# Squares of six output tiles added up on VectorE before the cross-partition sum, in a two-model transformer kernel

## The chip, the cores and the metric

The kernel runs on 1 core of one Trainium2 chip, in fp32 throughout. The metric is the device time in microseconds of one execution. Lower is better. The kernel before takes 3071.33 us (median of 3 runs, 3070.69 to 3072.82).

## What is computed

Two small transformer stacks of two layers each run one after the other on 256 latent and 256 context tokens with D = 1024. Their mixers are latent attention (MLA), a gated recurrence (HGRN2), an attention and pooling mixer ("even") and a neighbourhood attention ("odd"); their second halves are two SwiGLU feed-forwards and two mixtures of 32 experts. What matters here is what joins one half to the next. Every half ends in an output product, is gated into the residual stream x, and the next half begins with an RMS norm of x over the 1024 features:

```python
def rmsnorm(x, g):
    xf = x.astype(jnp.float32)
    y = xf * lax.rsqrt(jnp.mean(xf * xf, axis=-1, keepdims=True) + EPS)
    return (y * g.astype(jnp.float32)).astype(x.dtype)

x = x + g1 * y                                   # y: the mixer's output product
h2 = modulate_2(rmsnorm(x, norm_ffn_g[l]), sh2, sc2)   # h * (1 + scale) + shift
```

The mean of the squares is over all 1024 features of each token.

## The kernel before

The activations lie with features on the partitions: `X[:, k, :]` is feature tile k (128 features) of 8 (`KD = 8`) by up to 512 tokens (`T = 512`; `S = 256` is the latent half alone, `P = 128`). Summing squares over the features is then a sum over the partitions and over the 8 tiles. TensorE does both: a matmul of a matrix of ones (`ONES`) with the squared tile in `WORK[:, k * T:k * T + t]`, accumulated over k in PSUM bank 0.

`boundary` (L411) writes the join of two halves, as one part for each engine; it is called seven times. Six of the calls have a `product`, the output product of the half before; one (ahead of the odd mixer, after the first expert pass) has none. `tp` is the token width of the product, `t` that of the norm:

- MLA to feed-forward 1: tp 512, t 512
- feed-forward 1 to HGRN2: tp 512, t 512
- HGRN2 to feed-forward 2: tp 256, t 256
- feed-forward 2 to even mixer: tp 256, t 512 (the second model's context comes in here)
- even mixer to experts 1: tp 512, t 512
- odd mixer to experts 2: tp 256, t 256

They are called wide-wide (three times), narrow-narrow (twice) and narrow-wide (once) below.

The product runs over its weights in tiles of two input blocks (L451 is the matmul), eight PSUM banks being open at once, one for each output tile m. In the last weight tile (L475) m is the outer loop: two matmuls complete bank m and raise `product_made`. From then on four engines work in a chain for each m. VectorE (L517, one instruction per 256 tokens) gates the bank into `X[:, m]` and raises `added`. ScalarE (L491) squares `X[:, m]` into `WORK` and raises `squared`. TensorE (L460, `add_squares`) multiplies the square by `ONES`; that matmul for tile m - 2 is written into TensorE's program order behind the two product matmuls of tile m, for m of 2 to 7, and those of tiles 6 and 7 come last. The matmul for tile 7 raises `summed`. Then ScalarE takes the square root (L493), VectorE the reciprocal (L523) and the scaling of the eight tiles (L527), ScalarE adds the shift (L498), and TensorE starts on the next half as each normalised tile is `normed`. All engines execute their own instructions in order. SyncE waits for `product_made` to reach 8 and then issues the next half's loads (`rest`: L569, L1496, L1072, L1921 and behind it L2039); in the two expert joins GpSimd waits for it too.

Of the kernel before, what the change touches and what calls it, by code (L numbers as in the profile page):

```python
# [10 lines left out]
ALU = mybir.AluOpType  # L11
# [7 lines left out]
KD = D // P  # L19
S = 256  # L20
T = 2 * S
# [140 lines left out]
def build(nc, io, out):  # L162
    act_, dve_, pe_ = nc.scalar, nc.vector, nc.tensor
# [8 lines left out]
    WORK = sb("WORK", [P, KD * T])  # L172
# [27 lines left out]
    def sig(name):  # L200
        if name not in signals:
            signals[name] = Signal(nc, name)
        return signals[name]
# [3 lines left out]
    for name in ("inputs_in", "stored", "dve_step", "act_step", "squared", "summed", "rooted", "normed",  # L207
                 "silu_made", "h_made", "drained", "projected",
                 "scored", "peaked", "exped", "shared", "flipped", "turned", "weighted", "carried",
                 "staged", "gated", "forgot", "logged", "summed_up", "decayed", "spread", "levelled",  # L210
                 "levels_ready", "kx_flipped", "kx_copied", "state_made", "state_copied", "products",
                 "attended", "biased", "bias_in", "pooled", "pool_copied", "mixed",
                 "token_flipped", "token_copied", "routed", "group_exped", "second_exped", "ranked",
                 "rank_in", "picked", "gathered", "indices_made", "indexed", "rows_kept", "index_seen", "logits_kept", "logits_flipped", "expert_silu", "expert_h",
                 "pick_flipped", "pick_copied", "scattered", "added", "rounds_in",
                 "cleared", "mod_flipped", "inverted", "second_in", "cvec_in", "consts_in", "x_in", "late_in",
                 "silued", "chunk_made", "gained", "latent_made", "latent_squared", "latent_rooted", "latent_normed",
                 "latent_flipped", "latent_copied", "unit_made", "value_copied", "unit_squared", "unit_summed",
                 "unit_rooted", "unit_normed", "unit_flipped", "unit_copied", "mod_added",
                 "bounded", "q_made", "queried", "valued", "scanned", "level_exped", "read_in", "masked", "cross_made",  # L220
                 "cross_copied", "row_made", "row_kept", "row_squared", "row_summed", "row_rooted", "row_normed", "row_flipped", "row_copied",
                 "gains_in", "wide_in", "wide_silued", "dotted", "product_made", "out_squared", "out_rooted", "out_normed", "out_flipped", "out_copied",
                 "chunk_in0", "chunk_in1", "chunk_in2", "chunk_in3",
                 "xg_copied", "h_flipped", "h_copied", "y_copied", "weighed"):
        sig(name)
# [5 lines left out]
    def passed(**counts):  # L231
        for name, n in counts.items():
            signals[name].passed(n)
# [177 lines left out]
    def boundary(product, gain, layer, shift, scale, t, free, rest, sides=()):  # L411
# [3 lines left out]
        def of(name, n):  # L415
            return signals[name].sem, at[name] + n
# [29 lines left out]
        def pe_part(pe):  # L446
            def multiply(s, i, turn, first):
                pe.wait_ge(*of(f"loaded{s}", 16 * (turn + 1)))
                for r in range(2):
                    for m in range(KD):  # L450
                        last = pe_.matmul(PB[:, m, 0:tp], tile(s, 2, D)[:, r, m * P:(m + 1) * P],  # L451
                                          src(2 * i + r), start=first and r == 0, stop=False)
                last.then_inc(used[s].sem, 1)

            def add_squares(k):
                if product or k % 2 == 0:
                    pe.wait_ge(*of("squared", k + 1 if product else k // 2 + 1))
                else:
                    pe.wait_ge(*of("staged", k // 2 + 1))
                last = pe_.matmul(PB[:, 0, 0:t], ONES, WORK[:, k * T:k * T + t], start=k == 0, stop=k == KD - 1)  # L460
                if k == KD - 1:
                    last.then_inc(sig("summed").sem, 1)

            if product:
                multiply(0, 0, 0, True)
                with pe.Fori(0, pairs) as i:
                    for j in range(2):
                        multiply((1 + j) % 2, 2 * i + 1 + j, i + (1 + j) // 2, False)
                for i in tail[:-1]:
                    multiply(i % 2, i, i // 2, False)  # L470
                i = n_tiles - 1
                pe.wait_ge(*of(f"loaded{final}", 16 * (i // 2 + 1)))
                for m in range(KD):
                    for r in range(2):
                        last = pe_.matmul(PB[:, m, 0:tp], tile(final, 2, D)[:, r, m * P:(m + 1) * P],  # L475
                                          src(2 * i + r), start=False, stop=r == 1)
                    last.then_inc(sig("product_made").sem, 1)
                    if m >= 2:
                        add_squares(m - 2)
                add_squares(KD - 2)  # L480
                add_squares(KD - 1)
            else:
                for k in range(KD):
                    add_squares(k)
# [16 lines left out]
        def dve_part(dve):  # L501
            for share in side_shares(sides):
                side_dots(dve, of, sides, share, 0, 11)
            if not product:
                for k in range(1, KD, 2):
                    dve_.tensor_tensor(WORK[:, k * T:k * T + t], X[:, k, 0:t], X[:, k, 0:t], ALU.mult) \
                        .then_inc(sig("staged").sem, 1)
            for w in range(streams):
                last = dve_.scalar_tensor_tensor(
                    out=GAIN[:, w, :], in0=MODS[:, layer, KD * scale:KD * scale + KD, w], scalar=1.0, in1=gain,  # L510
                    op0=ALU.add, op1=ALU.mult)
            last.then_inc(sig("gained").sem, 1)
            if product:
                for m in range(KD):
                    dve.wait_ge(*of("product_made", m + 1))
                    for c in range(tp // S):
                        last = dve_.scalar_tensor_tensor(  # L517
                            out=X[:, m, half(c)], in0=PB[:, m, half(c)], scalar=piece(gate_layer, gate, m, c),
                            in1=X[:, m, half(c)], op0=ALU.mult, op1=ALU.add)
                    last.then_inc(sig("added").sem, 1)  # L520
            dve.wait_ge(*of("gained", 1))
            dve.wait_ge(*of("rooted", 1))
            dve_.reciprocal(ROOT[:, 0, 0:t], ROOT[:, 0, 0:t]).then_inc(sig("inverted").sem, 1)  # L523
            dve.wait_ge(*of("inverted", 1))
            for k in range(KD):
                for w in range(streams):
                    last = dve_.scalar_tensor_tensor(out=A[:, k, half(w)], in0=X[:, k, half(w)], scalar=GAIN[:, w, k:k + 1],  # L527
                                                     in1=ROOT[:, 0, half(w)], op0=ALU.mult, op1=ALU.mult)
                last.then_inc(sig("spread").sem, 1)
# [12 lines left out]
        for s in range(2 if product else 0):  # L542
            count = (n_tiles + 1 - s) // 2
            used[s].passed(count - (s == final))
            loaded[s].passed(16 * count)
        passed(product_made=KD if product else 0, added=KD if product else 0, squared=KD if product else KD // 2,
               staged=0 if product else KD // 2, summed=1, rooted=1, gained=1, inverted=1, spread=KD, normed=KD)
        return Boundary(sp_part, pe_part, act_part, dve_part, ready, multiplied)

# [1873 lines left out]
    def nothing(sp):  # L2423
# [3 lines left out]
    opening(mla_early)  # L2427
    product = mla(0)
    product = feed_forward(boundary(product, vec("norm2", 0, KD), 0, 3, 4, T, feed_free((1, 2)), feed_rest(w13[0], (1, 2))),
                           w13[0], w2[0], 0, T, sides=(1, 2))  # L2430
    product = hgrn2(boundary(product, vec("norm1", KD, 2 * KD), 1, 0, 1, T, hgrn2_head(1), hgrn2_head(0),
                              (1, 2)), 1)
    product = feed_forward(boundary(product, vec("norm2", KD, 2 * KD), 1, 3, 4, S, feed_free((3,)),
                                    feed_rest(w13[1], (3,), True)), w13[1], w2[1], 1, S, True, sides=(3,))
    product = even_mixer(boundary(product, vec("mix", 0, KD), 2, 0, 1, T, even_free, even_rest, (3,)), 2)
    experts(boundary(product, vec("ffn", 0, KD), 2, 3, 4, T, nothing, experts_early(0)), 2, 0, T, True)
    product = odd_mixer(boundary(None, vec("mix", KD, 2 * KD), 3, 0, 1, T, nothing, odd_early), 3)
# [109 lines left out]
```

## Time and profile before

| what | value |
|---|---|
| median of 3 runs | 3071.33 us (3070.69 to 3072.82) |
| the profiled execution | 3070.39 us, of which the span is 3068.6 us |
| granted TensorE clock, mean of the span | 0.968 |
| TensorE busy | 2847.9 us (93%), 12390 instructions |
| VectorE busy | 1163.6 us (38%) |
| ScalarE busy | 701.3 us (23%) |
| L475, the last weight tile of the six products | 192 matmul records |
| L460, the sums of squares of the seven joins | 112 matmul records |

An fp32 matmul appears as two records, so L460's 112 records are 56 matmuls: 8 in each of seven joins. In the timeline a row gives start, length, engine, line, what is written and read, how many instructions are merged into it and, in brackets, how long the engine was idle before and what released it. "PEld" rows are weight loads of TensorE, "SPq" rows are DMA issues of SyncE. The granted clock is 1.00 for 2.4 GHz and 0.50 for 1.2 GHz.

### The profile page before, as it was taken

Reading aid. Unit: us, or ns where it says so; the run is one execution under the profiler, and the core shown is the slowest. Engines: PE = TensorE matmul, PEld = TensorE weight load, DVE = VectorE, ACT = ScalarE, POOL = GpSimd, SP = SyncE. Lnnn points to the kernel's source line nnn. Section 1 sums busy time; section 2 is a strip of 40 time slices with the busy share of each in tenths; the row PEclk is TensorE's granted clock in tenths of the full one; section 3 lists DMA queues with packets and bytes.
Section 4 is the critical chain, followed back from the end, with each engine's and each line's share of the span. In section 5 each row is a group of like instructions: output and inputs, shape, how many; then the busy total and the mean of one; then the engine's idle time right before and its main releaser. Section 6 shows DMA issues by size and latency. Waiting matters only on the chain. (4 is left out here: it accounts for less than half of the span.)

```text
span 3068.6 us, 34189 instructions
## 1 busy us (share of the span) xinstructions
PE 2847.9 (93%) x12390; PEld 1568.3 (51%) x12390; DVE 1163.6 (38%) x2597; ACT 701.3 (23%) x1331; POOL 20.1 (1%) x26
## 2 busy tenths in 40 slices
PE   5999999999999988999989799999979979999997
PEld 3545444444467767887553333333347764444443
DVE  2322387770256664762232333323334322112222
ACT  2333200000155541001151112112123222112121
POOL 0000000000000000000000000000000000000000
PEclk9979999999999988999999899999999989999999
DMA  6122365551222105774003899999912249999993
GB/s 250 71 97 109 145 239 226 225 219 69 110 83 71 68 1 191 304 269 164 14 11 133 330 396 394 391 396 398 364 55 90 95 161 403 398 392 400 397 399 135
DMA packets 101826, 664.39 MB, mean 217 GB/s; under 512 B 10608, under 2 KB 19056, under 8 KB 25072
## 3 DMA queue, kind: packets, MB, share of 16 engines
q1 hardware_dynamic: 98576, 651.74, 54.3%
q0 software_dynamic: 2592, 9.44, 0.8%
q10 hardware_dynamic: 576, 2.10, 0.2%
q8 instruction: 54, 0.88, 0.1%
q14 instruction: 28, 0.23, 0.0%
HBM read 660.09 MB, written 3.15 MB: 216 GB/s over the span
## 5 line engine op out<-in xcount | busy, mean ns | idle before, releaser
L618 PE MATMUL PB<-A,RING 128*128 128x512 f32 (+1 forms) x1408 | 458.4, 489 | 9.8 <-ACT A L498 6.2
L618 PEld LDWEIGHTS PB<-A,RING 128*128 128x128 f32 x1408 | 269.3, 191 | 199.0 <-issue 174.7
L400 DVE SCALAR_TENSOR_TENSOR WORK<-RING,MORE 128x1024 f32<-128x1024 f32 x288 | 335.5, 1220 | 21.1 <-ACT MORE L632 11.8
L451 PE MATMUL PB<-BIG,RING 128*128 (+2 forms) x928 | 310.7, 497 | 5.5 <-PEq L586 3.3
L2293 DVE TENSOR_TENSOR BIG<-BIG,PB 64x512 f32<-64x512 f32 x64 | 44.2, 690 | 711.1 <-ACT BIG L2207 711.1
L2138 PE MATMUL PB<-BIG 128*128 128x512 f32 (+1 forms) x544 | 213.3, 515 | 49.1 <-DVE X L2300 45.6
L451 PEld LDWEIGHTS PB<-BIG,RING 128*128 128x128 f32 x928 | 175.9, 190 | 139.2 <-issue 128.6
L2106 PE MATMUL PB<-RING,BIG 128*64 128x512 f32 x1024 | 227.7, 597 | 0.0
L2300 DVE SCALAR_TENSOR_TENSOR X<-PB,MODS,X 128x256 f32<-128x256 f32 x408 | 176.6, 479 | 42.7 <-PE PB L2138 40.7
L2138 PEld LDWEIGHTS PB<-BIG 128*128 128x128 f32 x544 | 90.9, 190 | 184.6 <-DVE X L2300 107.3
L517 DVE SCALAR_TENSOR_TENSOR X<-PB,MODS,X 128x256 f32<-128x256 f32 x72 | 32.6, 480 | 357.7 <-PE PB L475 357.7
L2106 PEld LDWEIGHTS PB<-RING,BIG 128*64 128x64 f32 x1024 | 72.4, 138 | 138.2 <-issue 137.8
L2207 ACT ACTIVATE BIG<-PB 64x512 f32<-64x512 f32 x64 | 37.7, 589 | 364.9 <-PE PB L2106 364.9
L1596 PE MATMUL PB<-A,RING 128*128 128x512 f32 x256 | 114.5, 602 | 6.2 <-ACT A L498 6.2
L2218 ACT ACTIVATE BIG<-PB 64x512 f32<-64x512 f32 x128 | 75.8, 592 | 193.7 <-PE PB L2126 192.9
L2126 PE MATMUL PB<-RING,BIG 128*64 128x512 f32 x512 | 116.9, 598 | 1.8
L491 ACT ACTIVATE WORK<-X 128x512 f32<-128x512 f32 (+1 forms) x52 | 29.0, 563 | 390.6 <-DVE X L517 390.6
L637 ACT ACTIVATE RS<-PB 128x512 f32<-128x512 f32 (+1 forms) x44 | 21.6, 491 | 420.7 <-PE PB L618 420.7
L2126 PE MATMUL PB<-A,BIG 128*64 128x512 f32 x512 | 116.9, 598 | 0.0
L2106 PE MATMUL PB<-MORE,BIG 128*64 128x512 f32 x512 | 115.4, 592 | 0.0
L2106 PE MATMUL PB<-CST,BIG 128*64 128x512 f32 x256 | 115.4, 592 | 0.0
L2106 PE MATMUL PB<-BIG 128*64 128x512 f32 x256 | 115.1, 592 | 0.0
(350 smaller groups left out, 3387.0 us busy)
## 6 DMA issues: line engine op xcount, KB each, us to landing
RING<-moe_w SPq DMA_DIRECT2D x192, 1024.0 KB, 8.3
RING<-ada_rows SPq DMA_DIRECT2D x72, 1024.0 KB, 6.8
RING<-ffn_w SPq DMA_DIRECT2D x66, 1024.0 KB, 4.8
MORE<-moe_w SPq DMA_DIRECT2D x64, 1024.0 KB, 8.8
A<-moe_w SPq DMA_DIRECT2D x64, 1024.0 KB, 7.4
CST<-moe_w SPq DMA_DIRECT2D x32, 1024.0 KB, 8.9
BIG<-moe_w SPq DMA_DIRECT2D x32, 1024.0 KB, 10.8
RING<-ada_w SPq DMA_DIRECT2D x17, 1024.0 KB, 6.4
```

What stands on the lines that cost most here:

```text
L400: dve_.scalar_tensor_tensor(out=JUNK[:, n % 4, :], in0=RING[:, s, b * D:(b + 1) * D], scalar=1.0, in1=WIDE[:, side // 2, w, :], op0=ALU.mu ...
L451: last = pe_.matmul(PB[:, m, 0:tp], tile(s, 2, D)[:, r, m * P:(m + 1) * P], src(2 * i + r), start=first and r == 0, stop=False)
L517: last = dve_.scalar_tensor_tensor(out=X[:, m, half(c)], in0=PB[:, m, half(c)], scalar=piece(gate_layer, gate, m, c), in1=X[:, m, half(c)] ...
L618: last = pe_.matmul(PB[:, 2 * s + j, 0:t], tile(s, KD, P, j * KD * P)[:, k, :], A[:, k, 0:t], start=k == 0, stop=k == KD - 1)
L1596: last = pe_.matmul(PB[:, 1 + d, :], w[:, k, :], A[:, k, :], start=k == 0, stop=k == KD - 1)
L2106: last = pe_.matmul(PB[m * CAP:(m + 1) * CAP, 0, :], XGT[:, b, k, slots_of(e % 2)], spot_tile(s, 4, T)[:, k % 4, :], start=k == 0, stop=k ...
L2126: last = pe_.matmul(PB[m * CAP:(m + 1) * CAP, 2, :], HB[:, e % 2, k, :], spot_tile(s, 2, D)[:, k % 2, m * T:(m + 1) * T], start=k == 0, st ...
L2138: pe_.matmul(PB[:, 6 + m % 2, 0:t], Y2[:, b, m * P:(m + 1) * P], SWT[:, 0:t], start=True, stop=True) \
L2207: act_.activation(HS[CAP:P, e % 2, :], PB[0:CAP, 0, :], ACT.Silu).then_inc(sig("expert_silu").sem, 1)
L2218: last = act_.activation(Y2[slots_of(e % 2), b, m * T:(m + 1) * T], PB[m * CAP:(m + 1) * CAP, 2, :], ACT.Copy)
L2293: dve_.tensor_tensor(HS[0:CAP, j, :], HS[CAP:P, j, :], PB[CAP:P, 0, :], ALU.mult) \
L2300: last = dve_.scalar_tensor_tensor(out=X[:, m, half(w)], in0=PB[:, 6 + m % 2, half(w)], scalar=piece(2 + moe, 5, m, w), in1=X[:, m, half(w ...
```

## The change

In joins with a product, VectorE adds the squared tiles 0 to 5 up in place, in `WORK[:, 0:t]`, by five `tensor_tensor` adds. The add in step m (m of 2 to 6) comes behind L517 of tile m; it waits for the square of tile m - 1 and for the add before it, and raises `piled`. TensorE no longer has any sum of squares between the product matmuls. Behind the last of them it waits for the fifth `piled`, multiplies the pile by `ONES`, and then squares 6 and 7 as before. The join without a product is as it was.

```diff
             def add_squares(k):
-                if product or k % 2 == 0:
+                if k == 0 and product:
+                    pe.wait_ge(*of("piled", KD - 3))
+                elif product or k % 2 == 0:
                     pe.wait_ge(*of("squared", k + 1 if product else k // 2 + 1))
                 else:
                     pe.wait_ge(*of("staged", k // 2 + 1))
@@
                     last.then_inc(sig("product_made").sem, 1)
-                    if m >= 2:
-                        add_squares(m - 2)
+                add_squares(0)
                 add_squares(KD - 2)
                 add_squares(KD - 1)
@@
                     last.then_inc(sig("added").sem, 1)
+                    if 2 <= m < KD - 1:
+                        dve.wait_ge(*of("squared", m))
+                        dve.wait_ge(*of("piled", m - 2))
+                        dve_.tensor_tensor(WORK[:, 0:t], WORK[:, 0:t], WORK[:, (m - 1) * T:(m - 1) * T + t], ALU.add) \
+                            .then_inc(sig("piled").sem, 1)
```

The rest of the diff adds the semaphore `piled` to the list of names and counts its 5 steps in `passed`.

## Rows read from the trace of the kernel before

**Rows 1.** The page, part 1: busy time and share of the span.

```profile
PE 2847.9 (93%) x12390; PEld 1568.3 (51%) x12390; DVE 1163.6 (38%) x2597; ACT 701.3 (23%) x1331; POOL 20.1 (1%) x26
```

**Rows 2.** The page, part 5: L517, busy, mean ns, idle before and its releaser.

```profile
L517 DVE SCALAR_TENSOR_TENSOR X<-PB,MODS,X 128x256 f32<-128x256 f32 x72 | 32.6, 480 | 357.7 <-PE PB L475 357.7
```

**Rows 3.** Timeline, first wide-wide join (all engines).

```profile
336.99 5.31 PE L475 MATMUL PB<-BIG,RING 128*128 128x512 f32 x12
...
345.57 1.88 PE L475 MATMUL PB<-BIG,RING 128*128 128x512 f32 x4
...
347.29 1.02 PE L460 MATMUL PB<-WORK,CST 128*128 128x512 f32 x2
...
355.01 2.92 PE L460 MATMUL PB<-WORK,CST 128*128 128x512 f32 x6
...
355.22 0.87 DVE L517 SCALAR_TENSOR_TENSOR X<-PB,MODS,X 128x256 f32<-128x256 f32 x2 [1.70 <-PE PB L475]
...
356.12 0.63 ACT L491 ACTIVATE WORK<-X 128x512 f32<-128x512 f32 x1 [1.95 <-DVE X L517]
356.80 0.30 PEld L460 LDWEIGHTS PB<-WORK,CST 128*128 128x128 f32 x2 [0.74 <-ACT WORK L491]
357.97 0.69 ACT L493 ACTIVATE RS<-PB,CST 128x512 f32<-128x512 f32 x1 [1.22 <-PE PB L460]
358.76 3.35 DVE L523 RECIPROCAL RS<-RS 128x512 f32<-128x512 f32 x1 [2.67 <-ACT RS L493]
```

**Rows 4.** Waits of SyncE's DMA queue, whole span: total us, times, longest.

```profile
SPq L1921 <- PE PB L475: 47.0, 2, 31.4
SPq L569 <- PE PB L475: 43.8, 2, 29.1
SPq L1496 <- PE PB L475: 29.6, 1, 29.6
SPq L1072 <- PE PB L475: 14.9, 1, 14.9
```

**Rows 5.** Timeline, second narrow-narrow join (all engines).

```profile
2499.80 0.48 DVE L517 SCALAR_TENSOR_TENSOR X<-PB,MODS,X 128x256 f32<-128x256 f32 x1 [21.69 <-PE PB L475]
...
2500.66 0.48 DVE L517 SCALAR_TENSOR_TENSOR X<-PB,MODS,X 128x256 f32<-128x256 f32 x1 [0.38 <-PE PB L475]
...
2502.82 0.48 DVE L517 SCALAR_TENSOR_TENSOR X<-PB,MODS,X 128x256 f32<-128x256 f32 x1 [0.81 <-PE PB L475]
...
2504.12 0.48 DVE L517 SCALAR_TENSOR_TENSOR X<-PB,MODS,X 128x256 f32<-128x256 f32 x1 [0.81 <-PE PB L475]
...
2507.80 1.03 PE L460 MATMUL PB<-WORK,CST 128*128 128x256 f32 x4
...
2508.99 0.70 PE L460 MATMUL PB<-WORK,CST 128*128 128x256 f32 x2 [0.16 <-ACT WORK L491]
```

**Rows 6.** Timeline, first narrow-narrow join: start of the next half.

```profile
1200.62 7.57 PE L618 MATMUL PB<-A,RING 128*128 128x256 f32 x26 [3.67 <-DMA RING<-ffn_w]
```

**Rows 7.** Timeline, narrow-wide join.

```profile
1432.82 1.02 PE L460 MATMUL PB<-WORK,CST 128*128 128x512 f32 x2
...
1436.27 2.74 PE L460 MATMUL PB<-WORK,CST 128*128 128x512 f32 x6
```

**Rows 8.** Timeline of VectorE: adds and products of two tensors, elsewhere.

```profile
408.59 0.69 DVE L647 TENSOR_TENSOR BIG<-PB,RS 128x512 f32 x1 [1.36 <-ACT RS L637]
409.19 1.22 DVE L400 SCALAR_TENSOR_TENSOR WORK<-RING,MORE 128x1024 f32<-128x1024 f32 x1
...
1212.94 0.42 DVE L647 TENSOR_TENSOR BIG<-PB,RS 128x256 f32 x1 [0.36 <-DVE WORK L400]
1213.29 1.22 DVE L400 SCALAR_TENSOR_TENSOR WORK<-RING,MORE 128x1024 f32<-128x1024 f32 x1
...
2260.81 2.50 DVE L506 TENSOR_TENSOR WORK<-X 128x512 f32<-128x512 f32 x4 [4.06 <-PEq L2372]
```

**Rows 9.** Busy by stretch after two joins; columns: length, engines, PEclk, DMA, GB/s.

```profile
366.00:368.00 2.00, 2.00 (x4) 0.96 (x3) 2.00 (x6) 2.00 (x6) 0.00 (x0) 0.50 0.32 135
368.00:370.00 2.00, 2.00 (x5) 0.76 (x4) 0.57 (x2) 1.98 (x5) 0.00 (x0) 0.88 0.00 0
...
1198.00:1200.00 2.00, 0.00 (x0) 0.00 (x0) 1.96 (x3) 0.13 (x1) 0.00 (x0) 1.00 0.99 406
```

More of the change, by code:

```diff
@@ L221, in build @@
                  "cross_copied", "row_made", "row_kept", "row_squared", "row_summed", "row_rooted", "row_normed", "row_flipped", "row_copied",
-                 "gains_in", "wide_in", "wide_silued", "dotted", "product_made", "out_squared", "out_rooted", "out_normed", "out_flipped", "out_copied",
+                 "gains_in", "wide_in", "wide_silued", "dotted", "product_made", "piled", "out_squared", "out_rooted", "out_normed", "out_flipped", "out_copied",
                  "chunk_in0", "chunk_in1", "chunk_in2", "chunk_in3",
@@ L545, in boundary @@
             loaded[s].passed(16 * count)
-        passed(product_made=KD if product else 0, added=KD if product else 0, squared=KD if product else KD // 2,
+        passed(product_made=KD if product else 0, added=KD if product else 0, piled=KD - 3 if product else 0, squared=KD if product else KD // 2,
                staged=0 if product else KD // 2, summed=1, rooted=1, gained=1, inverted=1, spread=KD, normed=KD)
```

## Prediction

> **What bounds the kernel now.** Read the busy shares first. TensorE is busy for 93% of the span and the other engines for 38% or less [rows 1]. So time taken out of TensorE's own order counts where nothing else ends later, and the joins must be read one by one. L517 is the next view: all its idle time, 357.7 us, ended with TensorE's product [rows 2]. VectorE is early at every join and TensorE sets the pace.
>
> The timeline of a join shows that pace. In the wide-wide join, four records of L475 (two matmuls) take from 345.57 to 347.29, that is 0.43 us a record and 0.86 us for a matmul of 512 columns [rows 3]. The product's last tile begins at 336.99 and its last matmul gives way to L460 at 355.01 [rows 3]: 18.02 us, or 21 matmuls of 0.86. Sixteen are the product; five are squares 0 to 4. Those five lie ahead of the event that everything waits for. The squares 5 and 6, started at 355.01, lie beside L517 and L491 of tile 7 and cost nothing: the weight load for square 7 waits for ScalarE until 356.80, after 0.74 us of idle loading [rows 3].
>
> The next half hangs on that event too. SyncE's issues L569, L1496, L1072 and L1921 (L2039, the experts' weights, stands behind L1921) all waited for L475 [rows 4]. So transfers move with the product's end, and no stream of loads has a fixed start that would swallow the gain.
>
> **The change part by part.** *Removed from the path:* five matmuls in each of six joins. Wide-wide: 5 x 0.86 = 4.3 us, three times, 12.9 us. Narrow-narrow: without a square two L517 stand 0.86 us apart (2499.80, 2500.66), with one 1.30 us (2502.82, 2504.12) [rows 5]; a 256-column square is 0.43 to 0.44 us. 5 x 0.43 = 2.15 us, twice, 4.3 us. Narrow-wide: its squares are 512 columns wide. From 1432.82 to 1436.27, two rounds of two narrow product matmuls (0.86) and one square (0.86), 3.45 us, bear this out [rows 7]. 4.3 us. Sum: 21.5 us. The squares left behind the product are still three (pile, 6, 7) where they were three (5, 6, 7).
>
> *Added on VectorE:* five adds in each of the six joins, from and to SBUF. Durations: a two-tensor instruction of 512 columns takes 0.69 us, of 256 columns 0.42 [rows 8]. What counts is how soon the next can start. L400, behind L647 and with waits of its own that had been met, started 0.60 us after it (408.59, 409.19) in the wide case and 0.35 us after it in the narrow one (1212.94, 1213.29); four L506 of 512 columns from SBUF took 2.50 us, so 0.60 apart [rows 8]. Two L517 of 0.48 us (mean 480 ns [rows 2]) took 0.87 [rows 3], so they start 0.39 to 0.40 apart. I take these spacings (0.60, 0.35, 0.40) and not the full lengths, since L400 is in the same position as L517 behind the new add: another kind of instruction, a satisfied wait ahead of it.
>
> VectorE per tile against TensorE per tile, once the squares are out:
> - Wide-wide: 2 x 0.40 + 0.60 = 1.40 us against 2 x 0.86 = 1.72. TensorE still sets the pace. The fifth add begins 0.2 + 0.8 = 1.0 us after tile 6 is made (L517 starts 0.2 us behind its matmuls, 355.22 against 355.01 [rows 3]) and ends at 1.7, as tile 7 is made. TensorE's wait then costs 0.05 to 0.1 us for the event and 0.1 for the weight load, and the pile and square 6 end 1.85 to 1.9 us after the product's end. Square 7 could not start before 356.80 - 355.01 = 1.8 us plus its load [rows 3]. Cost on the path: 0.
> - Narrow-narrow: 0.40 + 0.35 = 0.75 against 0.86. The fifth add ends 0.2 + 0.4 + 0.42 = 1.0 us after tile 6 is made, 0.16 after tile 7. The pile starts some 0.3 us late, pile and square 6 end at 0.3 + 0.86 = 1.2 us, and square 7 cannot start before 2508.99 - 2507.80 = 1.19 us [rows 5]. Cost: 0, with nothing to spare.
> - Narrow-wide: 0.40 + 0.60 = 1.00 against 0.86. Here VectorE becomes the bound. It falls 0.14 us back per tile. L517 of tile 6 starts 0.2 + 4 x 0.14 = 0.76 us after its tile is made, the add 0.4 later, ends 0.69 later, and TensorE starts 0.15 behind that: 2.0 us after tile 6, 1.15 us after tile 7 is made. Then come the pile and square 6 (1.72 us) and square 7 (1.02 us with its drain), 3.89 us after the product's end where now it is 2.74 [rows 7]. Cost: 1.15 us, so this join gains 3.15.
>
> *The waits:* the add in step m waits for the square of tile m - 1, and L517 of tile m + 1 is queued behind it. ScalarE ends that square 0.90 + 0.63 = 1.53 us after L517 of tile m - 1 began (355.22 to 356.12, and 0.63 long) [rows 3]; the wide-wide add is not reached before 1.72 + 0.80. In the narrow-wide join L517 has half the length, so the square ends 1.15 us after it began and the add is reached at 1.40. Both waits are met before. The wait on the add before is older still. No DMA is issued, moved or removed.
>
> *Downstream:* in the first narrow-narrow join the next half began with the landing of its weights (L618 released by DMA at 1200.62 [rows 6]); that transfer is issued at the product's end and moves with it, by the full 2.15 us.
>
> **Sum:** 12.9 + 4.3 + 3.15 = 20.35 us. The profiled execution took 3070.39 us (span 3068.6 plus 1.8 around it), 0.94 below the median, so by it 3050.0; from the median, 3071.33 - 20.35 = 3051.0. I predict the latter.
>
> **The clock** can move this by chance. TensorE is idle while VectorE makes the reciprocal, and afterwards works at 1.2 GHz (0.50) for some time: in the first join until within 368 to 370 us [rows 9]. In the first narrow-narrow join the clock was still 1.00 in idle time (1198 to 1200) [rows 9]. Where the fall and rise lie against the work changes when the work moves; a slow stretch longer or shorter by 2 us costs or gives 1 us at each of six joins. My estimate of the sum is 3 us either way. The new idle in the narrow-wide join (1.15 us) is shorter than idle that left the clock whole.
>
> **The rivals.**
> - *VectorE is held until each instruction has ended.* Then the periods are 0.88 + 0.04 + 0.69 + 0.04 = 1.65 us (wide-wide), 0.98 (narrow-narrow) and 1.25 (narrow-wide). Wide-wide loses 0.1 us; narrow-narrow falls 0.12 us back per tile, 0.6 us at tile 7; in the narrow-wide join the pile starts 2.28 us after the product, a cost of 2.3. Gain 12.6 + 3.1 + 2.0 = 17.7, time 3053.6 us. Against it: 0.60 and 0.35 us from start to start [rows 8], though none of those instructions reads what the one before last wrote. This is also a rule of the Trainium skill, "VectorE: DVE Perf Modes", section "The DRAIN you can't avoid": the next instruction does not start until the pipeline is empty, with or without semaphores. By that rule the time is 3053.6 us; the trace, with 0.60 us against a length of 0.69, does not agree.
> - *The adds cost far more than their rows (slower).* The accumulation in place in `WORK`, while ScalarE writes and TensorE reads other parts of it, might be much slower than L506. The price goes by the slowest row of this width, the reciprocal's 3.35 us [rows 3], some 1.75 us if half as wide. VectorE per tile is then 4.15, 2.15 and 3.75 us; the pile would start 12.5, 6.7 and 14.8 us after the product, and the joins would lose 8.0, 4.3 and 10.5 us net: 43 us in all, 3114 us. It decides against the change where an add costs some 1.1 us more than its row. For it speaks only that no row adds in place; against it every two-tensor row of 512 columns I read, from PSUM or SBUF.
> - *The gain is given back in the expert passes.* If their weight stream set their end from a start before the product, the gains of the last two joins (4.3 + 2.15) would be hidden, 3057.5 us, and by the same reasoning at more joins under 0.2% would be left. Against it L2039 stands behind L1921, which waits for the product [rows 4].
>
> **How the numbers follow.** Measurement can tell about 0.2% (6 us) from no change. Forecast 0.70 (3051.0), held VectorE 0.17 (3053.6), gain given back 0.09 (3057.5 for 0.04 of it, less than 6 us gained for 0.05), slow adds 0.04 (3114). Faster 0.91, same 0.05, slower 0.04. The range takes in 20.35 us and 17.7 us with 3 us of clock on the far side of each, and a little of the rest: 3046.5 to 3057.5.
>
> **What would show it.** L460 should fall from 112 records to 52. In the wide-wide joins L475 should be one row of 32 records, 13.7 us long, with L460 directly behind it and VectorE's adds 0.69 us long; L517 of tile 7 should begin 0.2 us behind the product. In the narrow-wide join TensorE should be idle about 1.15 us ahead of the pile. L517 spaced over 0.9 us in the narrow-narrow joins would show VectorE held. Idle before L460 of over a microsecond in the wide-wide joins would show the adds to be dearer; a longer idle before L618 or L2106 with DMA as the releaser, a gain given back.

## The result

The changed kernel takes 3052.0 us (median of 4 runs, 3051.63 to 3052.27), where the kernel before took 3071.43 beside it (4 runs): ratio 0.9933, 95% interval 0.9918 to 0.9949, 15.7 to 25.2 us less. (The ratio compares all runs of the two kernels, taken side by side, and need not be the quotient of the medians, here 0.9937.) The forecast was 3051.0. The profiled execution has a span of 3049.8 us.

**The page after**, parts 1 and 5, where [rows 1, 2] answer. L517 has become L518.

```profile
PE 2831.5 (93%) x12330; PEld 1557.8 (51%) x12330; DVE 1179.3 (39%) x2627; ACT 700.8 (23%) x1331; POOL 20.2 (1%) x26
...
L518 DVE SCALAR_TENSOR_TENSOR X<-PB,MODS,X 128x256 f32<-128x256 f32 x72 | 32.6, 481 | 322.4 <-PE PB L477 321.9
```

TensorE has 60 records fewer (30 matmuls) and 16.4 us less busy time, VectorE 30 instructions and 15.7 us more. Thirty matmuls fewer should be worth 21.5 us; in the six joins TensorE is indeed busy for 77.4 us instead of 98.4, and the difference to 16.4 lies ahead of the first join (299.9 us busy, before 297.2) and between the joins. VectorE's idle time ahead of the gating fell by 35.3 us: it waits less, but TensorE is still what it waits for.

**Timeline of the first wide-wide join**, all engines, where [rows 3] answer. L477 is the product, L525 the add, L462 the sum of squares, L494 the square root.

```profile
338.76 13.90 PE L477 MATMUL PB<-BIG,RING 128*128 128x512 f32 x32
...
349.26 0.88 DVE L518 SCALAR_TENSOR_TENSOR X<-PB,MODS,X 128x256 f32<-128x256 f32 x2 [0.24 <-PE PB L477]
350.05 0.68 DVE L525 TENSOR_TENSOR WORK<-WORK 128x512 f32<-128x512 f32 x1
...
350.97 0.88 DVE L518 SCALAR_TENSOR_TENSOR X<-PB,MODS,X 128x256 f32<-128x256 f32 x2 [0.24 <-PE PB L477]
352.50 2.91 PE L462 MATMUL PB<-WORK,CST 128*128 128x512 f32 x6
...
352.69 0.88 DVE L518 SCALAR_TENSOR_TENSOR X<-PB,MODS,X 128x256 f32<-128x256 f32 x2 [0.24 <-PE PB L477]
353.60 0.63 ACT L492 ACTIVATE WORK<-X 128x512 f32<-128x512 f32 x1 [1.09 <-DVE X L518]
354.28 0.30 PEld L462 LDWEIGHTS PB<-WORK,CST 128*128 128x128 f32 x2 [0.62 <-ACT WORK L492]
355.45 0.69 ACT L494 ACTIVATE RS<-PB,CST 128x512 f32<-128x512 f32 x1 [1.22 <-PE PB L462]
```

The product is one unbroken row of 32 records. The add begins 0.79 us after the first of its tile's two gating instructions, and VectorE is idle for 0.24 us before the next tile: it keeps up. The load for square 7 still waits for ScalarE (354.28), as at 356.80 before [rows 3], so the pile and square 6 lie beside VectorE and ScalarE and cost nothing. Start of the product tile to square root: 16.69 us, before 20.98.

**The narrow-wide join**, where [rows 7] answer:

```profile
1417.37 7.07 PE L477 MATMUL PB<-BIG,RING 128*128 128x256 f32 x32
...
1423.15 0.48 DVE L518 SCALAR_TENSOR_TENSOR X<-PB,MODS,X 128x256 f32<-128x256 f32 x1
1423.54 0.69 DVE L525 TENSOR_TENSOR WORK<-WORK 128x512 f32<-128x512 f32 x1
...
1424.14 0.48 DVE L518 SCALAR_TENSOR_TENSOR X<-PB,MODS,X 128x256 f32<-128x256 f32 x1
...
1425.28 2.84 PE L462 MATMUL PB<-WORK,CST 128*128 128x512 f32 x6 [0.84 <-DVE WORK L525]
...
1428.16 0.69 ACT L494 ACTIVATE RS<-PB,CST 128x512 f32<-128x512 f32 x1 [1.88 <-PE PB L462]
```

From the first add on no L518 has idle time before it: VectorE is the bound, with 0.99 to 1.00 us per tile (1423.15, 1424.14), and TensorE waits for the fifth add.

**The first narrow-narrow join and the start of the next half**, where [rows 5, 6] answer:

```profile
1180.64 7.07 PE L477 MATMUL PB<-MORE,RING 128*128 128x256 f32 x32
...
1186.03 0.48 DVE L518 SCALAR_TENSOR_TENSOR X<-PB,MODS,X 128x256 f32<-128x256 f32 x1
...
1186.89 0.48 DVE L518 SCALAR_TENSOR_TENSOR X<-PB,MODS,X 128x256 f32<-128x256 f32 x1
1187.29 0.42 DVE L525 TENSOR_TENSOR WORK<-WORK 128x256 f32<-128x256 f32 x1
...
1187.76 1.68 PE L462 MATMUL PB<-WORK,CST 128*128 128x256 f32 x6
...
1189.48 0.47 ACT L494 ACTIVATE RS<-PB,CST 128x256 f32<-128x256 f32 x1 [0.79 <-PE PB L462]
...
1193.01 3.33 PE L624 MATMUL PB<-A,RING 128*128 128x256 f32 x7 [3.57 <-ACT A L499]
```

The gatings begin 0.86 us apart (1186.03, 1186.89), TensorE's pace. L624's matmul (L618 before) is released by ScalarE here, and not by DMA as in [rows 6]; the second profile of the kernel before, below, has ScalarE there too, so this difference is not the change's doing.

All six joins, from the start of the product's last weight tile to the start of the square root, in us, each worked out from two timeline rows:

| join | before | after | gain | forecast |
|---|---|---|---|---|
| wide-wide 1, 2, 3 | 20.98, 20.98, 20.99 | 16.69 each | 4.29, 4.29, 4.30 | 4.3 each |
| narrow-narrow 1, 2 | 10.99, 10.99 | 8.84 each | 2.15 each | 2.15 each |
| narrow-wide | 13.97 | 10.79 | 3.18 | 3.15 |
| sum | 98.90 | 78.54 | 20.36 | 20.35 |

The spans differ by 18.8 us, the medians by 19.4. The rest lies outside the joins: in these two profiles the stretch ahead of the first join, in which nothing was changed, is 336.99 us before and 338.76 after.

### The profile page after: what moved, and what is told of

The parts are those of the page before. It is cut to its first block and busy times, and to the rows that moved or that the text cites. A ratio compares the mean times of both kernels' runs of the same rounds, so it can differ in the third digit from the quotient of the medians.

```text
span 3049.8 us, 34130 instructions
## 1 busy us (share of the span) xinstructions
PE 2831.5 (93%) x12330; PEld 1557.8 (51%) x12330; DVE 1179.3 (39%) x2627; ACT 700.8 (23%) x1331; POOL 20.2 (1%) x26
## 3 DMA queue, kind: packets, MB, share of 16 engines
HBM read 660.09 MB, written 3.15 MB: 217 GB/s over the span
## 5 line engine op out<-in xcount | busy, mean ns | idle before, releaser
L624 PE MATMUL PB<-A,RING 128*128 128x512 f32 (+1 forms) x1408 | 458.8, 489 | 9.8 <-ACT A L499 9.8
L624 PEld LDWEIGHTS PB<-A,RING 128*128 128x128 f32 x1408 | 269.5, 192 | 199.1 <-issue 174.8
L400 DVE SCALAR_TENSOR_TENSOR WORK<-RING,MORE 128x1024 f32<-128x1024 f32 x288 | 335.6, 1222 | 21.5 <-ACT MORE L638 11.3
L518 DVE SCALAR_TENSOR_TENSOR X<-PB,MODS,X 128x256 f32<-128x256 f32 x72 | 32.6, 481 | 322.4 <-PE PB L477 321.9
```

Of the source, the lines that this page charges most:

```text
L400: dve_.scalar_tensor_tensor(out=JUNK[:, n % 4, :], in0=RING[:, s, b * D:(b + 1) * D], scalar=1.0, in1=WIDE[:, side // 2, w, :], op0=ALU.mu ...
L518: last = dve_.scalar_tensor_tensor(out=X[:, m, half(c)], in0=PB[:, m, half(c)], scalar=piece(gate_layer, gate, m, c), in1=X[:, m, half(c)] ...
L624: last = pe_.matmul(PB[:, 2 * s + j, 0:t], tile(s, KD, P, j * KD * P)[:, k, :], A[:, k, 0:t], start=k == 0, stop=k == KD - 1)
```

## The experiments

"Stretches" below are the times from one join's square root to the next join's last weight tile, the sixth being the one to the end; the stretch ahead of the first join is kept apart. "Half-clock time" is worked out from the view of busy time by stretch, in pieces of 20 us: length times two times (1 - granted clock), summed, which is the time at 1.2 GHz.

### The same two kernels again

> The kernel before, once more, for a second profile of the same program. What it tells apart: whether the stretches between the joins, in which the two kernels do the same work, repeat from one execution to the next. If the 1.0 us by which the measured gain (19.4 us) lies under the gain of the six joins (20.4 us) is chance of the clock in those stretches, then stretches of 200 to 800 us differ by 0.2 to 1.2 us between two profiles of this one kernel, in both directions. If the change itself costs something outside the joins, the stretches of this kernel repeat within 0.1 us and those of the changed kernel stand apart. Time: 3071 us.

> The changed kernel, once more, beside the others. Time 3052.0 us, ratio 0.9937. Each join from the start of the last weight tile to the square root as in the first profile: 16.69 us wide-wide, 8.84 us narrow-narrow, 10.79 us narrow-wide, to within 0.05 us, since nothing in a join depends on chance; the stretches between the joins by up to 1.2 us otherwise than in the first profile.

The six joins repeated within 0.02 us (sums 98.89 and 78.52). The changed kernel: 3050.9 us, ratio 0.9932 (0.9915 to 0.9949). The stretches repeated better than I expected, within 0.03 us for the changed kernel and 0.41 us for the kernel before, whose single execution here took 3076.25 us where I had expected 3071. What did not repeat is the stretch ahead of the first join: 336.99 and 342.02 us before, 338.76 and 339.23 after, 336.3 to 342.0 over all profiles taken, for the same instructions. The clock accounts for most of it. In the second profile of the kernel before, TensorE was busy at half clock for 48.9 us of this stretch, in the first for 39.9 (worked out from the trace's clock record and TensorE's rows). The length of the stretch less half of that time is 316.6 to 317.6 us in all 14 profiles. The kernel before took 3069.69 to 3075.86 us beside it on this chip. So a single comparison is uncertain by more than the 1 us that I wanted explained, and by ratio the gain is 20.6 and 20.9 us in the two measurements. There is no missing microsecond to explain in the times.

In the second profile of the kernel before, the half behind the first narrow-narrow join began 14.52 us after the product tile (first profile 14.63), and ScalarE released it:

```profile
1206.26 6.03 PE L618 MATMUL PB<-A,RING 128*128 128x256 f32 x19 [3.57 <-ACT A L498]
```

### Order alone

```diff
-                    if m >= 2:
-                        add_squares(m - 2)
-                add_squares(KD - 2)
-                add_squares(KD - 1)
+                for k in range(KD):
+                    add_squares(k)
```

> The kernel before, with all eight sums of squares on TensorE, but all of them behind the last product matmul; VectorE adds nothing. The matmuls are as many as before, the product ends 4.3 us (wide squares) or 2.15 us (narrow squares) earlier in its join, and with it the next half's transfers start earlier. My theory (five matmuls fewer are the whole gain): from the start of the last weight tile to the square root 24 matmuls in a row, 20.8 us wide-wide (before 20.98), 10.5 narrow-narrow (10.99), 13.95 narrow-wide (13.97); all in all 1.5 us less than before, about 3070 us. Rival (the gain comes from the product ending earlier, so that gating and transfers start earlier): up to 21 us less than before, 3050 us.

Measured 3063.5 us, ratio 0.9975 (0.9966 to 0.9985): 7.7 us less, neither of the two. In the joins my theory holds: 20.80, 20.81, 10.57, 13.98, 20.80 and 10.56 us, 97.52 in all, 1.4 less. The first of them in its timeline:

```profile
336.32 13.90 PE L475 MATMUL PB<-BIG,RING 128*128 128x512 f32 x32
...
350.05 7.03 PE L460 MATMUL PB<-WORK,CST 128*128 128x512 f32 x16
...
357.12 0.69 ACT L491 ACTIVATE RS<-PB,CST 128x512 f32<-128x512 f32 x1 [5.33 <-PE PB L460]
```

Another 6.0 us is gone from the stretches, more than half of it (3.3 us) from the second expert pass. There the granted clock differs: TensorE was busy at half clock for 10.1 us of that stretch instead of 17.7. The view by stretch, 30 us from the last join's square root on (columns as in [rows 9]), first of the kernel before:

```profile
2509.70:2519.70 10.00, 6.38 (x16) 2.66 (x16) 5.05 (x10) 3.80 (x10) 0.00 (x0) 0.66 0.97 388
2519.70:2529.70 10.00, 5.77 (x36) 5.38 (x37) 5.56 (x32) 3.88 (x6) 0.00 (x0) 0.80 1.01 425
2529.70:2539.70 10.00, 10.00 (x52) 5.83 (x53) 2.05 (x12) 2.48 (x3) 0.00 (x0) 0.86 1.01 417
```

and of this experiment:

```profile
2505.00:2515.00 10.00, 6.06 (x25) 3.21 (x26) 5.62 (x13) 4.09 (x10) 0.00 (x0) 0.83 1.00 420
2515.00:2525.00 10.00, 6.17 (x40) 5.85 (x39) 5.00 (x29) 4.12 (x6) 0.00 (x0) 0.83 1.02 424
2525.00:2535.00 10.00, 9.35 (x48) 3.96 (x46) 3.04 (x14) 2.47 (x3) 0.00 (x0) 1.00 1.01 417
```

0.66, 0.80 and 0.86 against 0.83, 0.83 and 1.00. But the transfers also start earlier against the square root here, so clock and transfers had to be told apart.

### The adds alone

```diff
                     last.then_inc(sig("added").sem, 1)
+                    if 2 <= m < KD - 1:
+                        dve.wait_ge(*of("squared", m))
+                        dve.wait_ge(*of("piled", m - 2))
+                        dve_.tensor_tensor(A[:, 0, 0:t], WORK[:, (m - 2) * T:(m - 2) * T + t], WORK[:, (m - 1) * T:(m - 1) * T + t], ALU.add) \
+                            .then_inc(sig("piled").sem, 1)
```

> The kernel before with its eight sums of squares where they were, and the five adds on VectorE beside them, of two squared tiles each, written to a place that nobody reads, with the waits of the change. It prices the adds without the gain. My theory: they are hidden at every join, since VectorE needs 1.40, 0.75 and 1.00 us per tile where TensorE with its squares needs 2.58, 1.30 and 1.72: 3071 us, within 0.5 us of before. Rival (the adds slow the chain, by traffic in the same memory or by holding back the gating of the next tile): at least 0.2 us at each of 30 adds, 6 us, 3077 us or more.

Measured 3072.8 us, ratio 1.0004 (0.9994 to 1.0013), and the joins take 98.92 us against 98.90. The rival's 6 us are excluded: an add beside a product that leaves VectorE time costs nothing.

### One kind of join at a time

```diff
+        piling = bool(product) and tp == t      # or: tp != T
-                if k == 0 and product:
+                if k == 0 and piling:
```

(and in the same way for the order of the squares and for VectorE's adds)

> The changed kernel, but the narrow-wide join (feed-forward 2 to even mixer) is as it was before: no adds, squares between the product matmuls. My sum gives this join 3.15 us of the gain: 3052.0 + 3.2 = 3055.2 us, and the join takes 13.97 us again. If VectorE held there as in the rival (each instruction ends before the next begins), the join would be worth 2.0 us: 3054.0 us.

> The changed kernel, but the three wide-wide joins are as they were before. My sum gives them 3 x 4.3 = 12.9 us: 3052.0 + 12.9 = 3064.9 us. If part of the gain of a join is lost again downstream (in the expert pass behind the third of them, say), they are worth less: 3060.6 us if the third is worth nothing.

Without the narrow-wide join the ratio is 0.9943 (0.9928 to 0.9958), 3.4 us more than the changed kernel's 0.9932; the median is 3053.4 us where I had expected 3055.2. The join takes 13.98 us again. The time alone could not tell 3.2 from 2.0 us; the join's own length does. Without the wide-wide joins it is 0.9968 (0.9956 to 0.9980), 11 us more where 12.9 were expected (median 3061.3 us, expected 3064.9). Those joins are back at 20.98, 20.98 and 20.99 us, all of the 12.9; the stretches are 3.3 us shorter than in the changed kernel, 0.8 in the first expert pass and 0.7 in the second.

### VectorE's work doubled

```diff
+                        dve_.tensor_tensor(A[:, m, 0:t], WORK[:, (m - 1) * T:(m - 1) * T + t], WORK[:, (m - 1) * T:(m - 1) * T + t], ALU.add)
                         dve_.tensor_tensor(WORK[:, 0:t], WORK[:, 0:t], WORK[:, (m - 1) * T:(m - 1) * T + t], ALU.add) \
```

> The changed kernel with a second add of the same width in front of each of its five, written to a place that nobody reads, so that VectorE's work per tile grows by 0.60 us (512 columns) or 0.35 us (256). It tests by what rule VectorE falls behind. My theory (instructions begin 0.60, 0.40 and 0.35 us apart): wide-wide 2.00 us per tile against 1.72, the pile starts 1.7 us late and the join is 1.6 us longer than in the changed kernel; narrow-narrow 1.10 against 0.86, 1.2 us longer; narrow-wide 1.60 against 0.86, 3.0 us longer. Sum 4.8 + 2.4 + 3.0 = 10.2 us, 3062.2 us. Rival (held until the end of each): periods 2.4, 1.45 and 2.0 us, 3.9, 2.9 and 5.8 us longer than the changed kernel, 23 us in all, 3075 us.

The joins became 1.62 us (wide-wide), 1.0 (narrow-narrow) and 4.7 us (narrow-wide) longer, 11.6 in all. The first two are near my theory and far from the rival. The third missed. VectorE fell behind as expected, but TensorE then sat idle long enough to lose its clock, and the three sums ran at half speed (timeline, then the view by stretch, of this kernel):

```profile
1426.11 0.68 DVE L525 TENSOR_TENSOR A<-WORK 128x512 f32<-128x512 f32 x1
...
1426.71 0.68 DVE L526 TENSOR_TENSOR WORK<-WORK 128x512 f32<-128x512 f32 x1
1427.31 0.47 DVE L518 SCALAR_TENSOR_TENSOR X<-PB,MODS,X 128x256 f32<-128x256 f32 x1
...
1429.04 4.54 PE L462 MATMUL PB<-WORK,CST 128*128 128x512 f32 x6 [3.84 <-DVE WORK L526]
```

```profile
1429.00:1431.00 2.00, 1.96 (x3) 0.94 (x4) 0.38 (x1) 0.63 (x1) 0.00 (x0) 0.56 1.03 430
```

4.54 us for six records that took 2.84 in the changed kernel. The starts (1426.11, 1426.71, 1427.31) are 0.60 us apart. The whole kernel was only 2.8 us slower than the changed one by ratio (3053.7 us, 0.9941, 0.9926 to 0.9956; expected 3062.2): 11.6 us lost in the joins, 8.4 given back in the stretches. One piece of it is the stretch behind the first narrow-narrow join, 226.27 us against 227.90: it had no half-clock time at all where the changed kernel had 3.6 us. Another is in the first expert pass, a wait for DMA of 7.35 us where the changed kernel has 10.05 (shown in the next experiment).

### Transfers later

```diff
                 sp.wait_ge(*of("product_made", KD))
+                sp.wait_ge(*of("rooted", 1))
```

> The changed kernel, but SyncE issues the next half's transfers only when the square root has been taken, 3.5 us (wide) or 2.2 us (narrow) later against the join; every other instruction is where it was. It prices the start of the transfers by itself, since the kernel with its squares behind the product came out 6 us faster than its joins explain. My theory now: in the expert passes the path follows the transfers at least in part, so that they end 2 to 5.7 us later in all (3.5 and 2.2 us at most), and the first narrow-narrow join, whose weights landed 0.1 us ahead of need, becomes 2.1 us longer: 3055 to 3060 us. Rival (transfers are hidden everywhere but at that join, and the 6 us were the clock's): 3053 us.

Measured 3058.7 us, ratio 0.9960 (0.9946 to 0.9974), 8.6 us above the changed kernel's ratio and at the upper end of the theory. The joins are unchanged (78.52 us). Behind the first narrow-narrow join TensorE waited for DMA:

```profile
1192.41 4.21 PE L625 MATMUL PB<-A,RING 128*128 128x256 f32 x9 [5.51 <-DMA RING<-ffn_w]
```

5.51 us of idle against 3.57, so 1.94 of the 2.1 us expected. The second expert pass did not move at all (557.72 us, as in the changed kernel), though its transfers started 2.3 us later. So it does not follow the start of its transfers, and the 3.3 us that the order alone took from it were the clock's. The first pass became 3.6 us longer. In it TensorE waits for token rows that GpSimd gathers by DMA. First the changed kernel, then this one:

```profile
1692.82 1.97 PE L2083 MATMUL PB<-CST,BIG 128*128 128x128 f32 x8 [10.05 <-DMA BIG<-token_rows,INDEX]
```

```profile
1687.85 1.08 POOL L2023 DMA_INDIRECT BIG<-token_rows,INDEX  x1 [34.57 <-DMA token_rows<-BIG]
...
1697.04 1.97 PE L2084 MATMUL PB<-CST,BIG 128*128 128x128 f32 x8 [13.46 <-DMA BIG<-token_rows,INDEX]
```

The wait grew by 3.41 us, nearly all of the 3.6. The gather began 4.1 us after VectorE had made its last index (1683.77) and was released by the landing of the token rows that are written before it; in the changed kernel it began 0.4 us after the last index. The additional half-clock time lay on idle time: over TensorE's busy time alone it is 30.5 us here and 30.3 in the changed kernel. So in this pass the delay is that of the transfers.

### The clock held up

```diff
+            def keep_warm():
+                for _ in range(7 if t == T else 8):
+                    pe_.matmul(PB[:, 7, 0:t], ONES, CST[:, 0:t], start=True, stop=True)
```

called behind the last sum of squares of each join, in the changed kernel and in the kernel before.

> The changed kernel with 7 matmuls of constants (8 of 256 columns in the narrow joins) behind the last sum of squares of every join, into a bank that nobody reads, so that TensorE is not idle while VectorE makes the reciprocal. It prices the clock. In the profiles each of those idle times was followed by 6.8 us at 0.50 (3.4 and 6.5 in the narrow joins), 3.3 to 7.7 us of which lay on work. If the clock stays at 1.00, half of each overlap comes back: 2.6, 2.9, 1.6, 2.2, 1.9 and 3.3 us, 14.5 us in all with some of it hidden behind transfers in the expert passes: 3052 - 12 = 3040 us. If the clock falls all the same, or the dummy matmuls delay the next half: 3052 us or more.

> The kernel before with the same dummy matmuls. With the clock out of play, the difference to the changed kernel with dummy matmuls should be the joins' alone, 20.4 us in the profiles' sum of joins and, in the stretches between joins, within 0.3 us of nothing. If the stretches of before and after still differ by up to 1 us each, something other than the clock lies behind it. Time about 3060 us.

The changed kernel with them took 3039.8 us, ratio 0.9895 (0.9879 to 0.9912), some 11 us less than without; the kernel before took 3057.6 us, ratio 0.9955 (0.9938 to 0.9971), 13.8 us less. The view by stretch behind the first join, first of the changed kernel, then of the same with the dummy matmuls:

```profile
356.00:360.00 4.00, 0.00 (x0) 0.00 (x0) 3.73 (x2) 0.13 (x1) 0.00 (x0) 1.00 1.02 430
360.00:364.00 4.00, 2.41 (x3) 1.17 (x4) 4.00 (x12) 3.46 (x9) 0.00 (x0) 0.51 1.01 428
```

```profile
353.00:357.00 4.00, 4.00 (x10) 1.71 (x9) 2.81 (x1) 0.69 (x1) 0.00 (x0) 1.00 1.01 426
357.00:361.00 4.00, 3.83 (x10) 1.43 (x8) 3.96 (x10) 2.51 (x7) 0.00 (x0) 1.00 1.01 428
```

The clock stayed at 1.00 from the square root into the next half at all six joins, and at none did the next half begin later (22.83 or 22.84 us from the product tile in the wide-wide joins, as without).

With the six idle times out of play I had expected the stretches of the two to agree within 0.3 us. They do not: 2625.4 us after, 2618.7 before. The joins' gain is 20.38 us, the difference of the ratios 18.4. The stretches are read from one profile of each, the changed kernel's being the slowest of its four executions. By stretch the changed kernel is 1.70, 0.05, 0.02, 1.25, 1.54 and 2.21 us longer. The first of these is the clock, at another place: feed-forward 1 has an idle time of 1.89 us between its two loops, for the same releaser in both. First the kernel before with dummy matmuls, TensorE's timeline and then the view by stretch around it:

```profile
669.60 5.82 PE L451 MATMUL PB<-BIG,RING 128*128 128x512 f32 x13 [1.89 <-PEq L591]
```

```profile
668.00:672.00 4.00, 2.40 (x6) 1.24 (x7) 2.99 (x4) 1.91 (x3) 0.00 (x0) 1.00 0.59 172
672.00:676.00 4.00, 4.00 (x10) 1.73 (x10) 3.78 (x9) 0.00 (x0) 0.00 (x0) 1.00 0.52 221
```

And the changed kernel with dummy matmuls:

```profile
663.80 4.94 PE L451 MATMUL PB<-BIG,RING 128*128 128x512 f32 x7 [1.89 <-PEq L597]
```

```profile
662.00:666.00 4.00, 2.19 (x4) 1.01 (x5) 2.78 (x4) 2.08 (x3) 0.00 (x0) 0.89 0.48 176
666.00:670.00 4.00, 4.00 (x8) 1.70 (x7) 3.78 (x9) 0.00 (x0) 0.00 (x0) 0.69 0.53 225
```

The same idle time cost nothing in one and 1.7 us in the other (the stretch is 447.81 and 449.51 us). In the first expert pass (1.54 us) it is the wait for token rows, 14.15 us after and 11.97 before. The stretches' length, their half-clock time, the part of it in which TensorE was busy (worked out as for the stretch ahead of the first join) and that wait, in us:

| kernel | stretches | half-clock time | of it TensorE busy | wait for token rows |
|---|---|---|---|---|
| before | 2632.7 | 153.8 | 96.3 | 11.54 |
| changed | 2632.5 | 150.7 | 100.3 | 10.05 |
| order alone | 2626.7 | 136.3 | 90.7 | 7.92 |
| before, dummy matmuls | 2618.7 | 98.9 | 61.7 | 11.97 |
| changed, dummy matmuls | 2625.4 | 112.6 | 72.4 | 14.15 |

Half-clock time costs something only where TensorE is busy, and then half of itself. Between the last two that is 5.3 us, and the wait adds 2.2: 7.5 us, where 6.7 were measured. Between the kernel before and the order alone it is 2.8 + 3.6 = 6.4 us, where 6.0 were measured. In the order-alone kernel's first expert pass the shorter wait was mostly taken up by half-clock time on work (31.1 us for 26.4), so that the pass is only 1.2 us shorter. Against the kernels without dummy matmuls the same sum gives some 3 us more than was measured (16.9 for 14.0 in the kernel before); why is open.

### A version that beats both

```diff
+    def pile_up(dve, t, of):
+        for a, b, *waits in ((3, 5, ("staged", 3)), (2, 4, ("squared", 3)), (3, 7, ("staged", 4), ("piled", 1)),
+                             (2, 6, ("squared", 4), ("piled", 2)), (3, 2, ("piled", 4))):
+            for wait in waits:
+                dve.wait_ge(*of(*wait))
+            dve_.tensor_tensor(WORK[:, a * T:a * T + t], WORK[:, a * T:a * T + t], WORK[:, b * T:b * T + t], ALU.add) \
+                .then_inc(sig("piled").sem, 1)
```

It is called behind VectorE's squares at the join without a product and in the final norm; TensorE then sums tiles 0, 1 and the pile in tile 3.

> The changed kernel with the same idea at the join without a product and at the final norm: TensorE sums tiles 0, 1 and a pile of tiles 2 to 7, which VectorE has added up by five adds (two piles side by side, then one). In the kernel before, those two sums ran at half clock at first (8.8 and 5.1 us for 8 matmuls) and were the path. My theory: VectorE ends the pile some 3.7 us after its last square (wide), 2 us (narrow); TensorE works on tiles 0 and 1 meanwhile; 3 to 3.7 us less at the join, 2 to 2.7 us at the final norm, 3046.5 us. Rival (the clock is lower for longer because TensorE has less to do, and the half behind the join pays it): 1 to 2 us are given back, 3048 to 3049 us.

> Piles at all joins and the final norm, with the dummy matmuls: the fastest kernel that the runs point to. Piles everywhere measured 3044.4 us; less 12 us of clock if the dummy matmuls keep it up: 3032 us. If they do not, 3044 us.

The piles everywhere: 3044.4 us, ratio 0.9912 (0.9898 to 0.9925). The join without a product in its timeline, with TensorE's row for tiles 0 and 1, VectorE's five adds and the row for the pile:

```profile
2245.40 3.78 PE L470 MATMUL PB<-WORK,CST 128*128 128x512 f32 x4 [6.96 <-ACT WORK L502]
2245.78 3.26 DVE L416 TENSOR_TENSOR WORK<-WORK 128x512 f32<-128x512 f32 x5
...
2249.09 1.39 PE L495 MATMUL PB<-WORK,CST 128*128 128x512 f32 x2
2250.52 0.69 ACT L504 ACTIVATE RS<-PB,CST 128x512 f32<-128x512 f32 x1 [3.61 <-PE PB L495]
```

From ScalarE's table load to the square root it takes 7.2 us instead of the changed kernel's 11.4 (4.2 less, 3 to 3.7 expected), the final norm 13.4 instead of 15.2 (1.8 less, 2 to 2.7 expected). 1.3 us are given back in the odd mixer, as the rival had it, and the second expert pass is 1.2 us shorter. With the dummy matmuls: 3032.5 us (3030.55 to 3035.57), ratio 0.9872 (0.9855 to 0.9888), 39 us less than the kernel before and by ratio some 18 less than the changed kernel; 3032 was expected.

## Why the prediction was right

**The path.** That TensorE's own order sets the joins, and five matmuls lie ahead of the product's end at each, is shown by the table of joins and by the order-alone kernel, in which the same matmuls behind the product save only 1.4 us in the joins.

**VectorE's rate.** The choice of start-to-start spacings over lengths was the step that decided between 20.35 and 17.7 us, and the narrow-wide join shows it right: 0.40 and 0.59 to 0.60 us from start to start (1423.15, 1423.54, 1424.14), behind instructions of 0.48 and 0.69 us. The rival's narrow-narrow joins would have had gatings 0.98 us apart and a square root 0.6 us later; the square root is where it would be without adds. By the rule of the Trainium skill, "VectorE: DVE Perf Modes", section "The DRAIN you can't avoid", that the next instruction does not start until the pipeline is empty, the gain would have been 17.7 us; the trace does not agree, with a start 0.60 us behind that of an add of 0.69. The same section also says that a next instruction that is not held starts earlier, which the trace bears out; the forecast cited the rule without that sentence.

**The narrow-wide cost.** Forecast 1.15 us, measured 1.11 (4.29 - 3.18). TensorE's idle row says 0.84 us, since a row's end is modelled; the difference of starts is what counts.

**The narrow-narrow joins** had nothing to spare, and lost nothing: the pile started 0.25 us behind the product (0.3 forecast), with the square root unmoved.

**Downstream.** The gain was not taken back by the weight streams. It needs them to start at the product's end, as forecast: started at the square root instead, they cost 1.9 us at the first narrow-narrow join and 3.4 in the first expert pass. For the first narrow-narrow join, the forecast was 2.15 us and the next half began 2.26 earlier (14.63 to 12.37 us after the product tile). The 0.11 us are a DMA wait that only the first profile of the kernel before has: against the second (14.52) the gain is 2.15. So the forecast's reason, weights that land last there [rows 6], was a tie seen in one profile. In the last experiments the stretches gave back or took several microseconds, both ways, by the clock and by one DMA wait.

**What the forecast had too small.** I gave the clock 3 us, at six joins. The real scatter has three other parts that I did not read: the stretch ahead of the first join (5.7 us from the shortest to the longest profile), the clock around idle times inside the halves, and the wait for token rows in the first expert pass, 7.35 to 14.15 us in the kernels above. The last two gave 6.7 us between two kernels with equal work there. That the changed kernel's stretches came out equal to those of the kernel before (2632.5 and 2632.7 us) was luck: by the half-clock time on work they should be 2.0 us longer, by that wait 1.5 shorter. It is luck as to the forecast and not from run to run, since the second profiles have 2632.6 and 2633.5. My expectations for the order alone (off by 6 us), the wide-wide joins (2 us) and the doubled adds (7 us in the total, 1.7 in one join) left out the same terms.

One reading of the clock was wrong, though what followed from it held. The forecast took the idle time of 3.67 us in the first narrow-narrow join [rows 6] for one that left the clock whole, because the clock was still 1.00 within it [rows 9]. It fell when the work had begun again, in the kernel before:

```profile
1200.00:1202.00 2.00, 1.38 (x5) 1.17 (x6) 2.00 (x6) 2.00 (x6) 0.00 (x0) 0.83 1.01 426
1202.00:1204.00 2.00, 2.00 (x7) 1.53 (x6) 0.60 (x2) 1.98 (x4) 0.00 (x0) 0.50 1.02 430
```

The new idle time in the narrow-wide join did leave the clock at 1.00 (1424 to 1430 in the changed kernel), and after the longer one of the doubled adds, 3.84 us, the sums there ran at half clock.

Left open are what sets the wait for token rows from kernel to kernel (11.54 us before, 10.05 in the changed kernel, both repeated to 0.2 us), and what decides whether the clock falls behind a given idle time.

## What to carry to other kernels

A sum over partitions and tiles needs TensorE only once per pile: adding the tiles up on an engine that is idle beside a TensorE-bound loop gains the matmuls' full time, as long as that engine's starts per tile fit into TensorE's. Price a chain of VectorE instructions by the distance of starts in the trace, not by their lengths. Judge such a change by the joins' own lengths, which repeat to 0.02 us, before the total, in which the clock and a DMA wait move by several microseconds with every shift; and where TensorE must wait some microseconds, a few matmuls of constants into a free bank can keep its clock up (11 to 14 us less at six joins here).

## What the runs showed of the hardware

- VectorE starts a tensor add 0.40 us after a gating instruction of 0.48 us has started, and the next gating 0.60 us after an add of 0.69 us, across kinds of instruction and with satisfied semaphore waits between them.
- An add of 512 fp32 columns in place, SBUF to SBUF, takes 0.68 us, as does one that is not in place (`A<-WORK`, 1426.11 in the kernel with doubled adds).
- TensorE idle for 3.84 us came back at half clock (six records in 4.54 us for 2.84); after 1.89 us of idle the clock fell in one kernel and not in the other. Whether a given idle time costs anything is not a property of that idle time alone.
- After 3.67 us of idle the clock was still 1.00 when work began again, and 0.50 within 4 us of it (view above).
- The stretch ahead of the first join took 336.3 to 342.0 us in 14 profiles; less half of TensorE's busy time at half clock it is 316.6 to 317.6.
